# Value outputs at the end of the step, softmax scaling ahead of the next score read, and banks and pieces of the next projection dealt out anew

## The chip, the cores and the metric

The kernel runs on one core of a Trainium2 chip. The metric is device time in microseconds (us) of one execution, and lower is better. The kernel is one launch of hand-ordered instruction streams: TensorE (PE in the profile), VectorE (DVE), ScalarE (ACT), GpSimd (POOL) and the DMA queue of SyncE (SP). Each engine runs its own stream in order and waits on semaphores for the others.

## The reference

One layer of a hybrid attention block over 1024 frames of width 1024, then a SwiGLU and a last norm. Cut to what matters here:

```python
h = rmsnorm(x); proj = h @ w_in
# A: 4 heads, two softmax maps each; a = p0 - lam*p1; o = a @ v (v 128 wide)
# B: 8 heads of 64, band of 9 chunks of 64 keys; o = softmax(q k^T/8 + bias) @ v
# C: 8 heads of 64, causal, score += c_q - c_k; o = softmax(...) @ v
merged = sum_i sigmoid(gate_i) * (o_i @ w_br_i)
x = x + merged @ w_out
x = x + (silu(h2 @ w_gate) * (h2 @ w_up)) @ w_down
return rmsnorm(x)
```

All of it is float32. The kernel gets float32 precision out of TensorE by splitting each operand into a high and a low part (`_hi`, `_lo`) and adding three products (`three_passes`, L182 to L184).

## The kernel before, in words

The program is four blocks: norm, attention, merge and feed-forward. Only the attention block is touched. It runs 12 **units**: four of branch A (one head with its two maps each), four of B and four of C (two heads each). The units of A and of B are two bodies in a loop of two turns, those of C are written out.

Within a unit there are 16 **steps**. Step s has one query tile of 128 rows and one map or head. The four engines do this for step s:

- **TensorE** multiplies the scores of step s + 2 (L927, L928, in C also the mask, L930), turns the probabilities of step s by transposes through the identity (L956; in A only in odd steps), does some **pieces** of the next unit's projection (L182 to L184; a piece is 6 matmuls of 512 columns), and in even steps from 2 on multiplies by V (L972 and L974 in A, L993 and L994 in B and C).
- **VectorE** reads the scores out of PSUM with the bias added and the row's extreme (`read_scores`, L780; in C one more small operation, L789), divides the next step's probabilities by their sum (`scale_probs`, L811 and L813; in A instead `mix_maps`, L820 to L825, in even steps), and subtracts for the low part of the turned chunks (`chunks_low`, L798 and L801).
- **ScalarE** takes the high part of the turned chunks (`chunks_hi`, L663 and L665) and the exponentials of step s + 2 (`exp`, L650).
- The **value output** of a product by V is a copy on ScalarE (`o_low_a` L674, `o_low_bc` L682) and an addition on VectorE (`o_out_a` L836, `o_out_bc` L846). It comes in odd steps from 3 on.

The next unit's projection is 6 **groups** g0 to g5 of 4 pieces: g0 and g1 give K, g2 and g3 give Q, g4 and g5 give V. g0 is done ahead of step 0, the rest at the steps of `PIECES_AT`. `EVAC_AT` says at which step ScalarE (`project_out`) and, for K and Q, VectorE (`project_low`, L742 to L751) empty a group, and `SPLIT_AT` at which step ScalarE makes the high part of the next weight slab (`split_hi`, L616), after which GpSimd makes its low part (`split_lo`, L589). TensorE begins a group once its PSUM bank is free and its slab is split. Both waits stand in `piece`. The bank of a group is chosen in `proj_bank`; banks 0 and 1 hold the scores of even steps and 2 and 3 those of odd steps, and a step of 4 key tiles or fewer leaves the second bank of its pair unused.

In the loop of a step the value output stands first on both engines, and on VectorE the next score read stands ahead of the scaling (L865 to L878).

Of the kernel before, what the change touches and what calls it, by code (L numbers as in the profile page):

```python
# [32 lines left out]
P = 128  # L33
# [82 lines left out]
PIECES_AT = [2, 2, 2, 2, 0, 2, 2, 0, 2, 2, 0, 1, 1, 1, 1, 0, 0]  # L116
EVAC_AT = {0: 0, 2: 1, 4: 2, 7: 3, 10: 4, 16: 5}
SPLIT_AT = {0: 1, 5: 2, 10: 3}
# [298 lines left out]
def block_attention(nc, ps, keep, scratch, w_in_k, w_br_b):  # L417
    h_hi, h_lo, ident = keep["h_hi"], keep["h_lo"], keep["ident_r"][:, :].bitcast(F32)
    with ExitStack() as ctx:
# [23 lines left out]
        neg_max, shift, rowsum, rinv = (sb(n, [P, 4]) for n in ("neg_max", "shift", "rowsum", "rinv"))  # L443
# [32 lines left out]
        def proj_bank(unit, g):  # L476

            if isinstance(unit, int) and unit in (0, UNITS):
                return bank(ps, (0, 1, 2, 3, 5, 6)[g] if unit == 0 else 6)
            return bank(ps, (3, 1, 6, 6, 6, 6)[g])  # L480
# [131 lines left out]
        def _(act):  # L612
# [57 lines left out]
            def o_low_a(c, i):  # L670

                act.wait_ge(pv_chunk, c["chunks"] + chunks_through(0, 2 * i + 1))
                act.wait_ge(rinv_ready, c["outs"] + (i + 1))
                nc.scalar.activation(o_low[:, i % 2 * P:(i % 2 + 1) * P], pv_bank[:, P:2 * P], ACT.Copy,  # L674
                                     scale=rinv[:, 2 * (i % 2):2 * (i % 2) + 1]).then_inc(o_low_ready, 1)
# [8 lines left out]
            def unit_body(b, it, du, last=False):  # L684
# [7 lines left out]
                for s in range(STEPS + 2):  # L692
                    if b == 0 and s >= 3 and s % 2 == 1:
                        o_low_a(c, (s - 3) // 2)
                    if b > 0 and s >= 3 and s % 2 == 1:
                        o_low_bc(c, (s - 3) // 2)
# [16 lines left out]

# [21 lines left out]
        def _(dve):  # L735
# [79 lines left out]
            def mix_maps(c, i):  # L815
# [4 lines left out]
                nc.vector.reciprocal(rinv[:, q:q + 2], rowsum[:, q:q + 2]).then_inc(rinv_ready, 1)  # L820
                dve.wait_ge(rinv_ready, c["outs"] + (i + 1))
                nc.vector.tensor_scalar(ratio[:, i % 2:i % 2 + 1], rowsum[:, q:q + 1], rinv[:, q + 1:q + 2],
# [9 lines left out]
            def o_out_a(c, i):  # L832
                if i == 0:
                    heads_room(c)
                dve.wait_ge(o_low_ready, c["outs"] + (i + 1))
                nc.vector.scalar_tensor_tensor(out=heads[:, i * P:(i + 1) * P], in0=pv_bank[:, 0:P],  # L836
                                               scalar=rinv[:, 2 * (i % 2):2 * (i % 2) + 1], in1=o_low[:, i % 2 * P:(i % 2 + 1) * P],
                                               op0=ALU.mult, op1=ALU.add).then_inc(o_out, 1)
# [10 lines left out]
            def unit_body(b, it, du, project=True):  # L849
# [14 lines left out]
                for s in range(STEPS + 2):  # L864
                    if b == 0 and s >= 3 and s % 2 == 1:  # L865
                        o_out_a(c, (s - 3) // 2)
                    if b > 0 and s >= 3 and s % 2 == 1:
                        o_out_bc(c, (s - 3) // 2)
                    if b == 0 and s % 2 == 0 and s < STEPS:
                        mix_maps(c, s // 2)  # L870
                    if project and s in EVAC_AT:
                        project_low(c["unit"] + 1, EVAC_AT[s], 1 - du)
                    if s + 2 < STEPS:
                        read_scores(b, c, s + 2)
                    if b > 0 and s + 1 < STEPS:
                        scale_probs(b, c, s + 1)
                    if s in turns:
                        chunks_low(b, c, s)  # L878
# [15 lines left out]
        def _(pe):  # L894
            def piece(unit, n, slot):
# [6 lines left out]
                if part == 0 and not (isinstance(unit, int) and unit == 0):  # L902
                    pe.wait_ge(proj_out, 6 * unit + g)
# [6 lines left out]
            def score(b, c, s, last):  # L910
# [9 lines left out]
                if s == STEPS // 2 and not last:  # L920
                    pe.wait_ge(proj_out, 6 * c["unit"] + 8)
# [57 lines left out]
            def times_v_bc(b, c, g):  # L979
                i, m = 2 * (g // 2), g % 2  # L980
                first, n = keys_of(b, g)
                if g >= 2:
                    pe.wait_ge(o_out, c["outs"] + (g - 1))
                elif b == 1 and g == 0:
                    pe.wait_ge(o_out, c["outs"])
# [864 lines left out]
```

## Time and profile before

| | us |
|---|---|
| median of 3 runs | 2151.11 |
| lowest and highest of them | 2147.57 and 2158.26 |
| the profiled execution | 2156.16 |
| its span, first to last instruction | 2154.3 |
| TensorE busy in it | 1988.8 (92%) |
| VectorE busy | 999.7 (46%) |
| ScalarE busy | 710.8 (33%) |
| GpSimd busy | 94.5 (4%) |

The attention block lies between 86 and 917 us of the span. In the rows further down, a bracket at a row's end is the time for which the engine had stood idle before it, and the instruction of another engine whose end released it. Matmuls are pipelined: one of 512 columns is shown with 0.39 us although the next one starts 0.23 us after it, so the time that a wait costs is best read between starts of rows.

### The profile page before, as it was taken

The numbers are of one execution on the slowest core, as the hardware profiler recorded it, in microseconds if no ns is written. First come the engines' busy times: TensorE is split into PE (matmuls) and PEld (weight loads), VectorE is DVE, ScalarE is ACT, GpSimd is POOL, SyncE is SP. The second block draws the span as 40 slices with busy tenths as digits, with TensorE's granted clock in tenths as the row PEclk, the third lists the DMA queues.
The fourth block names the chain that finished last, engine by engine and source line by source line (L and its number), as shares of the span: only waits on it lengthen the run. The fifth ranks groups of instructions, "written<-read, shape, count | busy, mean of one in ns | idle before, by whom it ended". The sixth has DMA issues, their size and how long they took to land. (4 is left out here: it accounts for less than half of the span.)

```text
span 2154.3 us, 26265 instructions
## 1 busy us (share of the span) xinstructions
PE 1988.8 (92%) x9542; PEld 1647.9 (76%) x9542; DVE 999.7 (46%) x1950; ACT 710.8 (33%) x1310; POOL 94.5 (4%) x59
## 2 busy tenths in 40 slices
PE   7888988888888888899999999999999999999997
PEld 3777777777777777778787887878888888888886
DVE  4355555565556556732433225754333333333326
ACT  5344444554545445522233112241111111111122
POOL 1110100100100000000000000000000000000000
PEclk9999999999999999999999999999999999999998
DMA  6412222122212211031211113102111111111111
GB/s 218 127 50 50 75 64 61 43 50 61 68 49 50 69 53 31 30 118 44 83 45 53 49 44 147 59 20 59 59 49 31 47 49 58 49 49 29 49 59 78
DMA packets 145268, 133.32 MB, mean 62 GB/s; under 512 B 7476, under 2 KB 130484, under 8 KB 142888
## 3 DMA queue, kind: packets, MB, share of 16 engines
q1 hardware_dynamic: 141768, 132.16, 20.8%
q8 instruction: 44, 0.72, 0.1%
q10 hardware_dynamic: 3424, 0.17, 0.1%
q14 instruction: 32, 0.26, 0.0%
HBM read 109.17 MB, written 16.06 MB: 58 GB/s over the span
## 5 line engine op out<-in xcount | busy, mean ns | idle before, releaser
L182 PE MATMUL ps<-h_hi,w_hi 128*128 128x512 f32 x1664 | 674.3, 405 | 51.2 <-DVE k_stack L745 37.4
L184 PE MATMUL ps<-h_hi,w_lo 128*128 128x512 f32 x1664 | 658.9, 396 | 0.0
L183 PE MATMUL ps<-h_lo,w_hi 128*128 128x512 f32 x1664 | 658.8, 396 | 0.0
L182 PEld LDWEIGHTS ps<-h_hi,w_hi 128*128 128x128 f32 x1664 | 318.8, 192 | 121.9 <-DVE k_stack L745 37.0
L184 PEld LDWEIGHTS ps<-h_hi,w_lo 128*128 128x128 f32 x1664 | 318.7, 192 | 69.5
L183 PEld LDWEIGHTS ps<-h_lo,w_hi 128*128 128x128 f32 x1664 | 319.6, 192 | 62.0
L1598 DVE TENSOR_TENSOR residual<-residual,ps 128x512 f32<-128x512 f32 x240 | 162.6, 685 | 113.9 <-PE ps L184 109.2
L956 PE MATMUL ps<-ident_r,probs_bc 128*128 128x128 f32 x528 | 85.2, 285 | 51.9 <-DVE probs_bc L813 36.3
L1589 DVE TENSOR_TENSOR w_lo<-w_raw,w_hi 128x1024 fp32r<-128x1024 f32 x46 | 56.4, 1226 | 158.4 <-ACT w_hi L1491 158.4
L1499 ACT ACTIVATE bias<-ps 128x512 f32<-128x512 f32 x44 | 26.1, 594 | 311.5 <-PE ps L184 311.5
L184 PE MATMUL ps<-w_down_hi,act_lo 128*128 128x512 f32 x320 | 124.5, 389 | 0.0
L183 PE MATMUL ps<-w_down_lo,act_hi 128*128 128x512 f32 x320 | 124.5, 389 | 0.0
L182 PE MATMUL ps<-w_down_hi,act_hi 128*128 128x512 f32 x320 | 124.5, 389 | 0.0
L589 POOL TENSOR_TENSOR w_lo<-w_raw,w_hi 128x1024 fp32r<-128x1024 f32 (+1 forms) x36 | 85.2, 2368 | 723.0 <-ACT w_hi L616 690.3
L780 DVE CUSTOM_DVE_ANT_0 probs_bc<-ps,bias 128x640 f32<-128x640 f32 (+7 forms) x128 | 90.0, 703 | 53.5 <-PE ps L930 24.2
L956 PEld LDWEIGHTS ps<-ident_r,probs_bc 128*128 128x128 f32 x528 | 60.1, 143 | 66.4 <-DVE probs_bc L813 40.8
L1607 DVE TENSOR_TENSOR bias<-ps,bias 128x512 f32<-128x512 f32 x44 | 30.4, 691 | 167.2 <-PE ps L184 167.2
L665 ACT ACTIVATE probs_tb_hi<-ps 128x384 fp32r<-128x384 f32 (+2 forms) x192 | 82.6, 463 | 74.0 <-PE ps L956 72.6
L927 PE MATMUL ps<-k_stack,q_stack 128*128 128x320 f32 (+5 forms) x288 | 98.3, 345 | 0.0
L928 PE MATMUL ps<-k_stack,q_stack 128*128 128x320 f32 (+5 forms) x288 | 95.5, 335 | 0.0
L1504 ACT ACTIVATE act_hi<-bias 128x512 fp32r<-128x512 f32 x44 | 27.8, 632 | 202.9 <-DVE bias L1607 202.9
L801 DVE TENSOR_TENSOR probs_tb_lo<-ps,probs_tb_hi 128x384 fp32r<-128x384 f32 (+2 forms) x192 | 93.8, 516 | 2.1 <-ACT probs_tb_hi L665 1.7
(202 smaller groups left out, 2714.9 us busy)
## 6 DMA issues: line engine op xcount, KB each, us to landing
w_raw<-in_w_in SPq DMA_DIRECT2D x60, 512.0 KB, 3.8
w_raw<-in_w_gate_up SPq DMA_DIRECT2D x44, 512.0 KB, 3.7
k_stack<-k_stack SPq DMA_DIRECT2D x24, 512.0 KB, 6.4
w_raw<-in_w_down SPq DMA_DIRECT2D x22, 512.0 KB, 3.5
x_all<-in_x SPq DMA_DIRECT2D x8, 512.0 KB, 8.7
bias<-bias_a_scratch SPq DMA_DIRECT2D x4, 1024.0 KB, 5.9
heads_bc_scratch<-heads_out SPq DMA_DIRECT2D x8, 512.0 KB, 3.1
bias<-neg_c_scratch SPq DMA_DIRECT2D x4, 1024.0 KB, 5.3
```

The source lines that it names most:

```text
L182: nc.tensor.matmul(out, w_hi, x_hi, start=first, stop=False)
L183: nc.tensor.matmul(out, w_hi, x_lo, start=False, stop=False)
L184: return nc.tensor.matmul(out, w_lo, x_hi, start=False, stop=last)
L589: nc.gpsimd.tensor_tensor(w_lo[part], w_raw[part], w_hi[part].bitcast(F32), ALU.subtract).then_inc(w_split, 1)
L665: nc.scalar.activation(turned_place(ptb_hi, b, i, m, tile, size), turn_bank[lc % 2][:, 0:size * P].rearrange("p (t q) -> p t q", q=P), ACT ...
L780: nc.vector.tensor_tensor_reduce(out=row_view(probs_of(b, s)[:, 0:n * P], n), in0=scores_view(s, n), in1=row_view(window, n), scale=-1.0, ...
L801: nc.vector.tensor_tensor(turned_place(ptb_lo, b, i, m, tile, size), turn_bank[lc % 2][:, 0:size * P].rearrange("p (t q) -> p t q", q=P), ...
L927: nc.tensor.matmul(dst, q, k_st[:, par, 2 * m, keys], start=True, stop=False)
L928: last_one = nc.tensor.matmul(dst, q, k_st[:, par, 2 * m + 1, keys], start=False, stop=not diagonal)
L956: last = nc.tensor.transpose(turn_bank[lc % 2][:, x * P:(x + 1) * P], src[:, tile * P:(tile + 1) * P], ident[:, :])
L1589: nc.vector.tensor_tensor(w_lo[kind], w_raw[:, raw, :], w_hi[kind].bitcast(F32), ALU.subtract).then_inc(w_split, 1)
L1598: nc.vector.tensor_tensor(res[:, t, cols], res[:, t, cols], bank(ps, 4 + o % 4), ALU.add).then_inc(added, 1)
```

## The change

The arithmetic and the number of instructions on data stay as they are. What moves:

1. ScalarE's copy and VectorE's addition of the value output go from the head of an odd step to its end. `rinv` grows from 4 to 8 columns so that A's two reciprocals live long enough.
2. In B and C, VectorE scales the probabilities of step s + 1 ahead of reading the scores of step s + 2.
3. The groups g0 to g5 go to banks 3, 6, 1, 6, 6, 6 (before 3, 1, 6, 6, 6, 6), and a group waits only for the last group of its own bank to be emptied, where before it waited for all groups ahead of it.
4. Pieces, emptyings and slab splits are dealt out anew over the steps.
5. A product by V in B and C waits until the output just ahead of it is out (`outs + g`, before `outs + g - 1` from g = 2 on).

```diff
-PIECES_AT = [2, 2, 2, 2, 0, 2, 2, 0, 2, 2, 0, 1, 1, 1, 1, 0, 0]
-EVAC_AT = {0: 0, 2: 1, 4: 2, 7: 3, 10: 4, 16: 5}
-SPLIT_AT = {0: 1, 5: 2, 10: 3}
+PIECES_AT = [2, 2, 2, 2, 1, 1, 1, 1, 0, 1, 1, 1, 1, 1, 1, 2, 0]
+EVAC_AT = {0: 0, 2: 1, 4: 2, 8: 3, 13: 4, 16: 5}
+SPLIT_AT = {0: 1, 4: 2, 8: 3}
+PROJ_BANKS = (3, 6, 1, 6, 6, 6)
...
-        neg_max, shift, rowsum, rinv = (sb(n, [P, 4]) for n in ("neg_max", "shift", "rowsum", "rinv"))
+        neg_max, shift, rowsum = (sb(n, [P, 4]) for n in ("neg_max", "shift", "rowsum"))
+        rinv = sb("rinv", [P, 8])
...
-            return bank(ps, (3, 1, 6, 6, 6, 6)[g])
+            return bank(ps, PROJ_BANKS[g])
...
                 for s in range(STEPS + 2):
-                    if b == 0 and s >= 3 and s % 2 == 1:
-                        o_low_a(c, (s - 3) // 2)
-                    if b > 0 and s >= 3 and s % 2 == 1:
-                        o_low_bc(c, (s - 3) // 2)
...
                         split_hi(slab + j, odd % 2, 6 * b + 3 * it + odd // 2)
-
+                    if b == 0 and s >= 3 and s % 2 == 1:
+                        o_low_a(c, (s - 3) // 2)
+                    if b > 0 and s >= 3 and s % 2 == 1:
+                        o_low_bc(c, (s - 3) // 2)
...
                 for s in range(STEPS + 2):
+                    if b == 0 and s % 2 == 0 and s < STEPS:
+                        mix_maps(c, s // 2)
+                    if project and s in EVAC_AT:
+                        project_low(c["unit"] + 1, EVAC_AT[s], 1 - du)
+                    if b > 0 and s + 1 < STEPS:
+                        scale_probs(b, c, s + 1)
+                    if s + 2 < STEPS:
+                        read_scores(b, c, s + 2)
+                    if s in turns:
+                        chunks_low(b, c, s)
                     if b == 0 and s >= 3 and s % 2 == 1:
                         o_out_a(c, (s - 3) // 2)
                     if b > 0 and s >= 3 and s % 2 == 1:
                         o_out_bc(c, (s - 3) // 2)
-                    if b == 0 and s % 2 == 0 and s < STEPS:
-                        mix_maps(c, s // 2)
-                    if project and s in EVAC_AT:
-                        project_low(c["unit"] + 1, EVAC_AT[s], 1 - du)
-                    if s + 2 < STEPS:
-                        read_scores(b, c, s + 2)
-                    if b > 0 and s + 1 < STEPS:
-                        scale_probs(b, c, s + 1)
-                    if s in turns:
-                        chunks_low(b, c, s)
...
-                    pe.wait_ge(proj_out, 6 * unit + g)
+                    same = [x for x in range(g) if PROJ_BANKS[x] == PROJ_BANKS[g]]
+                    pe.wait_ge(proj_out, 6 * unit + (same[-1] + 1 if same else 0))
...
-                    pe.wait_ge(proj_out, 6 * c["unit"] + 8)
+                    pe.wait_ge(proj_out, 6 * c["unit"] + 9)
...
-                if g >= 2:
-                    pe.wait_ge(o_out, c["outs"] + (g - 1))
-                elif b == 1 and g == 0:
-                    pe.wait_ge(o_out, c["outs"])
+                pe.wait_ge(o_out, c["outs"] + g)
```

Two places show what stands in a row. The first is VectorE in the first B unit, from the end of step 6 to the low part of step 7. L813 is the scaling, L780 the score read, L801 the low part of turned chunks, L846 the value output, L748 and L751 the low part of g3 (Q). Before:

```order
L846 TENSOR_TENSOR heads_out<-ps,o_low 64x256 [waits o_low_ready]
L740 REGISTER_ALU
L748 SCALAR_TENSOR_TENSOR q_stack<-ps,q_stack 64x512 [waits proj_hi]
L750 REGISTER_ALU
L751 SCALAR_TENSOR_TENSOR q_stack<-ps,q_stack 64x512 [waits proj_hi]
L771 REGISTER_ALU
L780 ISA probs_bc,neg_max<-ps,bias 128x640 [waits scores_ready,chunk_turned]
L780 ISA neg_max 128x1
L811 RECIPROCAL rinv<-rowsum 128x1 [waits probs_ready]
L812 REGISTER_ALU
L813 TENSOR_SCALAR probs_bc<-probs_bc,rinv 128x640 [waits rinv_ready]
```

and now (lines from here on are numbered one to three higher in the changed kernel):

```order
L812 RECIPROCAL rinv<-rowsum 128x1 [waits probs_ready]
L813 REGISTER_ALU
L814 TENSOR_SCALAR probs_bc<-probs_bc,rinv 128x640 [waits rinv_ready]
L772 REGISTER_ALU
L781 ISA probs_bc,neg_max<-ps,bias 128x640 [waits scores_ready,chunk_turned]
L781 ISA neg_max 128x1
L797 REGISTER_ALU
L802 TENSOR_TENSOR probs_tb_lo<-ps,probs_tb_hi 128x4x128 [waits chunk_hi]
L847 REGISTER_ALU
L848 TENSOR_TENSOR heads_out<-ps,o_low 64x256 [waits o_low_ready]
L741 REGISTER_ALU
L749 SCALAR_TENSOR_TENSOR q_stack<-ps,q_stack 64x512 [waits proj_hi]
```

The scaling has moved from behind the value output, g3 and the score read to the head of the step; the value output has moved behind the chunks; and g3 belongs to step 8 now.

The second place is TensorE in the same unit at step 8: the transposes of step 8, then what comes ahead of the product by V. Before:

```order
L954 REGISTER_ALU
L956 MATMUL ps<-ident_r,probs_bc 128x128 [waits chunk_out]
L956 MATMUL ps<-ident_r,probs_bc 128x128
L901 REGISTER_ALU
L903 REGISTER_ALU [waits w_split]
L182 MATMUL ps<-h_hi,w_hi 128x512 [waits proj_out]
L183 MATMUL ps<-h_lo,w_hi 128x512
```

and now:

```order
L957 REGISTER_ALU
L959 MATMUL ps<-ident_r,probs_bc 128x128 [waits chunk_out]
L959 MATMUL ps<-ident_r,probs_bc 128x128
L985 REGISTER_ALU
L993 MATMUL ps<-probs_tb_hi,v_split 128x256 [waits chunk_out,o_out]
L994 MATMUL ps<-probs_tb_lo,v_split 128x256
```

The two pieces of step 8 are gone from there (one each has gone to steps 4 and 7, and the others moved along), so the product by V stands right behind the transposes.

## Rows read from the trace of the kernel before

**Rows 1.** Waits on TensorE: waiter, releaser, us in total, times, longest us.

```profile
PE ps L182 <- DVE k_stack L745: 37.4, 22, 1.9
PE ps L956 <- DVE probs_bc L813: 36.3, 21, 3.2
PE ps L956 <- DVE probs_tb_lo L801: 15.3, 17, 1.4
```

**Rows 2.** Windows: stretch, then PE, PEld, DVE, ACT, POOL busy, granted clock, DMA.

```profile
150.00:218.00 68.00, 60.57 (x314) 51.09 (x313) 36.87 (x86) 32.26 (x68) 7.43 (x4) 0.95 0.24 67
351.00:419.00 68.00, 57.40 (x331) 48.97 (x329) 40.34 (x106) 34.79 (x79) 7.59 (x5) 1.00 0.21 56
711.00:790.00 79.00, 67.29 (x370) 57.83 (x369) 47.09 (x122) 37.52 (x79) 7.16 (x3) 0.94 0.19 54
921.00:2154.00 1233.00, 1206.10 (x5328) 996.09 (x5328) 473.72 (x638) 262.30 (x358) 0.00 (x0) 0.99 0.19 57
```

**Rows 3.** Timeline of TensorE, first B unit: start us, us, then instruction.

```profile
354.48 0.30 PE L956 MATMUL ps<-ident_r,probs_bc 128*128 128x128 f32 x1
356.58 0.50 PE L182 MATMUL ps<-h_hi,w_hi 128*128 128x512 f32 x1 [1.80 <-DVE k_stack L745]
359.41 0.28 PE L927 MATMUL ps<-k_stack,q_stack 128*128 128x256 f32 x1
...
364.89 0.50 PE L182 MATMUL ps<-h_hi,w_hi 128*128 128x512 f32 x1 [1.65 <-DVE k_stack L745]
...
375.11 0.66 PE L956 MATMUL ps<-ident_r,probs_bc 128*128 128x128 f32 x4 [1.70 <-DVE probs_bc L813]
...
387.19 0.96 PE L956 MATMUL ps<-ident_r,probs_bc 128*128 128x128 f32 x5 [2.46 <-DVE probs_bc L813]
...
396.11 0.71 PE L956 MATMUL ps<-ident_r,probs_bc 128*128 128x128 f32 x5
396.58 0.37 PE L993 MATMUL ps<-probs_tb_hi,v_split 128*128 128x256 f32 x1
...
398.01 0.36 PE L927 MATMUL ps<-k_stack,q_stack 128*128 128x320 f32 x1
...
415.96 0.27 PE L927 MATMUL ps<-k_stack,q_stack 128*128 128x128 f32 x1
```

**Rows 4.** Timeline of VectorE, same unit, steps 6 and 7.

```profile
380.27 1.17 DVE L813 TENSOR_SCALAR probs_bc<-probs_bc,rinv 128x512 f32<-128x512 f32 x1
...
383.52 0.42 DVE L846 TENSOR_TENSOR heads_out<-ps,o_low 64x256 f32<-64x256 f32 x1 [1.62 <-ACT o_low L682]
...
385.56 0.82 DVE L780 CUSTOM_DVE_ANT_0 probs_bc<-ps,bias 128x640 f32<-128x640 f32 x1
...
386.50 0.55 DVE L813 TENSOR_SCALAR probs_bc<-probs_bc,rinv 128x640 f32<-128x640 f32 x1
```

**Rows 5.** Timelines of ScalarE and GpSimd, same unit.

```profile
357.29 1.04 ACT L616 ACTIVATE w_hi<-w_raw 128x1024 fp32r<-128x1024 f32 x1
386.42 0.83 ACT L650 ACTIVATE probs_bc<-probs_bc,neg_max 128x640 f32<-128x640 f32 x1 [1.08 <-DVE neg_max L780]
387.16 0.18 ACT L650 ACTIVATION_READ_ACCUMULATOR probs_bc<-probs_bc,neg_max 128x1 f32 x1
```
```profile
358.48 2.40 POOL L589 TENSOR_TENSOR w_lo<-w_raw,w_hi 128x1024 fp32r<-128x1024 f32 x1 [24.50 <-ACT w_hi L616]
...
378.76 2.40 POOL L589 TENSOR_TENSOR w_lo<-w_raw,w_hi 128x1024 fp32r<-128x1024 f32 x1 [17.37 <-ACT w_hi L616]
```

**Rows 6.** Timeline of VectorE in the third C unit, 8 key tiles.

```profile
844.17 1.21 DVE L780 CUSTOM_DVE_ANT_0 probs_bc<-ps,bias 128x1024 f32<-128x1024 f32 x1
...
845.42 0.27 DVE L789 TENSOR_SCALAR shift<-neg_max,c_col 128x1 f32<-128x1 f32 x1
```

**Rows 7.** Timeline of TensorE, last wait of the first A unit.

```profile
145.10 0.39 PE L972 MATMUL ps<-v_split,probs_ta_hi 128*128 128x256 f32 x1 [1.05 <-DVE probs_ta_lo L798]
```

**Rows 8.** Timeline of TensorE, last unit (C), a late wait.

```profile
907.90 1.05 PE L956 MATMUL ps<-ident_r,probs_bc 128*128 128x128 f32 x7 [1.43 <-DVE probs_tb_lo L801]
```

More of the change, by code:

```diff
@@ L674, in o_low_a @@
                 nc.scalar.activation(o_low[:, i % 2 * P:(i % 2 + 1) * P], pv_bank[:, P:2 * P], ACT.Copy,
-                                     scale=rinv[:, 2 * (i % 2):2 * (i % 2) + 1]).then_inc(o_low_ready, 1)
+                                     scale=rinv[:, 2 * (i % 4):2 * (i % 4) + 1]).then_inc(o_low_ready, 1)
             def o_low_bc(c, g):
@@ L819, in mix_maps @@
                 dve.wait_ge(probs_ready, c["step"] + (2 * i + 2))
-                nc.vector.reciprocal(rinv[:, q:q + 2], rowsum[:, q:q + 2]).then_inc(rinv_ready, 1)
+                r = 2 * (i % 4)
+                nc.vector.reciprocal(rinv[:, r:r + 2], rowsum[:, q:q + 2]).then_inc(rinv_ready, 1)
                 dve.wait_ge(rinv_ready, c["outs"] + (i + 1))
-                nc.vector.tensor_scalar(ratio[:, i % 2:i % 2 + 1], rowsum[:, q:q + 1], rinv[:, q + 1:q + 2],
+                nc.vector.tensor_scalar(ratio[:, i % 2:i % 2 + 1], rowsum[:, q:q + 1], rinv[:, r + 1:r + 2],
                                         keep["neg_lam"][:, :], ALU.mult, ALU.mult).then_inc(ratio_ready, 1)
@@ L836, in o_out_a @@
                 nc.vector.scalar_tensor_tensor(out=heads[:, i * P:(i + 1) * P], in0=pv_bank[:, 0:P],
-                                               scalar=rinv[:, 2 * (i % 2):2 * (i % 2) + 1], in1=o_low[:, i % 2 * P:(i % 2 + 1) * P],
+                                               scalar=rinv[:, 2 * (i % 4):2 * (i % 4) + 1], in1=o_low[:, i % 2 * P:(i % 2 + 1) * P],
                                                op0=ALU.mult, op1=ALU.add).then_inc(o_out, 1)
```

## The prediction

> **What bounds the kernel now.** I read three views in turn. The windows come first [rows 2]. From 921 us on TensorE is busy for 1206 of 1233 us, and nothing there is touched. In the attention block it is busy for only 57 of 68 us in a unit, while VectorE has 40 and ScalarE 35. No engine is full: the block is bound by chains of waits. The waits view names them [rows 1]. TensorE starts a projection group late because K of the group ahead is still being emptied (37.4 us), turns late because the probabilities aren't scaled (36.3), and waits for the low parts of the chunks turned ahead (15.3). The timeline of one B unit then shows the seven waits that each of the four B units has: 1.80 and 1.65 at the starts of g1 and g2, 1.70 and 2.46 at the transposes of steps 5 and 8 [rows 3], and further on 1.31, 0.35 and 1.34 at steps 12, 14 and 16, for low parts. They sum to 10.6 us by the brackets. Between starts a wait is some 0.2 longer: the transpose at 354.48 takes 0.06 to issue, and the next matmul starts at 356.58, so 2.04 are lost where the bracket says 1.80. A B unit thus loses about 12 us. By the same count an A unit loses 9 (7.4 by its brackets) and a C unit 13 (11.7).
>
> A second loss comes with them. The granted clock is 1.00 in the first B unit and 0.94 to 0.95 in the A and the C unit shown [rows 2]; 0.05 of 68 us is 3.4 us. 
>
> **Method.** I keep the durations of the rows and lay them along the new order of each engine, one unit of each kind. The latencies between engines come from the rows too: a score read of 640 columns and its accumulator take 0.83 and an exponential 0.92 until its sum is out [rows 4, 5]; a reciprocal and scaling take 0.74; a TensorE wait ends 0.14 after VectorE (386.50 + 0.55 to 387.19); two pieces take 2.83 (356.58 to 359.41).
>
> **Part 1, banks (change 3).** g1 no longer waits for g0. It starts at 354.54 instead of 356.58. g2 has bank 1 and waits for no group, so the 1.65 goes too. What is late next is the weight slab. ScalarE's high part comes after the exponential of step 2, whose score read now stands behind a scaling; that moves it from 357.29 to 358.05. GpSimd then works 2.40 us, until 361.65 [rows 5], and TensorE, ready at 361.0, starts g2 at 361.8: a new wait of 0.8. Net gain 3.1 in B. In A no scaling stands in front and the wait is 0.35, in C 0.65. Score(8) waits for one more group than before, which is emptied at step 4, and costs nothing.
>
> **Part 2, the middle of the unit (changes 1, 2 and 4).** At step 5 the 1.70 goes: one piece (1.45) now lies in front, and the scaling saves itself the score read (0.6 to 0.8). At step 8 the 2.46 goes for the same reasons, g3 being emptied one step later. But the new order makes a chain on VectorE and ScalarE: score read, exponential, scaling, next score read. One turn of it is 0.83 + 0.92 + 0.74 and 0.06 of signals, 2.55 us; in odd steps the value output hangs behind the exponential (copy 0.38, addition 0.43) and adds 0.84. A pair of steps takes 5.94. TensorE needs 6.3 for a pair with one piece in each (two scores 1.2, transposes 2 × 0.47 from 396.11 to 396.58, a product 1.43 from there to 398.01, pieces 2.8 [rows 3]). So the chain fits, with 0.4 to spare, except where something else is put in. At step 8 it is: g3 costs VectorE 1.4 and ScalarE 1.2, TensorE has no piece there, and the product now waits for the output just ahead of it (change 5). Laid out, B waits 0.65 at the product of step 6, 0.6 and 1.0 at step 8 (second chunk; product), and 2.0 at the transposes of step 9. From step 10 on it waits 0.1 in all.
>
> **Part 3, the end of the unit.** The 1.31 and 0.35 go because VectorE no longer stands still for the value output before the low parts. The 1.34 goes because two pieces (2.83) lie between the last transposes and the last product, which needs only some 2.2.
>
> **Sum for B:** new waits 0.8 + 0.65 + 0.6 + 1.0 + 2.0 + 0.1 = 5.1 for 12.1, a gain of 7.0 a unit, 28 for four.
>
> **C:** the chain is longer. At 8 tiles the read with its shift is 1.52 [rows 6], the exponential 1.26 and the scaling 0.96; a pair of such steps takes 8.4, and TensorE needs at most 8.1 for its own pair, so there the chain leads. New waits: 0.65, 0.5, 0.9 + 1.05 at step 8, 2.1 at step 9, then 0.3, 0.15, 0.3 and 1.45 at step 14, in all 7.4 for 13.2. Gain 6, for three units 18. **The last unit** has few pieces, and VectorE and ScalarE set its pace already; a late wait for a low part there is 1.43 [rows 8]. There the longer chain shows: its last exponential comes some 3 us later. I take −2.5.
>
> **A:** there is no scaling in A; only the value output moves. It has a single PV bank, so each product waits for the output ahead of it, which now comes after the low part and an exponential instead of before them. With one piece a step the cover is thinner. I lay out 0.35 (slab), 0.3, 1.6 at step 8, 0.85 for g4 (its bank is freed at step 8 now), 1.8 at step 10, 0.25, 2.0 for g5 at step 13 (ScalarE empties g4 behind an exponential), 0.1: 7.2 for 9. The last wait, 1.05 for the low part [rows 7], goes, the middle pays. Gain 2, for four units 8.
>
> **Clock:** the waits at g1 go, which start 7 of the 17 falls. But the new waits lie close together at steps 8 to 10, and I expect a fall there in most units. From 17 to about 14: +4. The bounds are +20 (hardly any fall left) and −10 (two in each unit).
>
> Together: 28 + 18 − 2.5 + 8 + 4 = 55.5 us. The profiled execution (2156.2) would become 2100.7; it lies 5 above the median, so the forecast is 2151.1 − 55.5 = **2095.6**. Errors of 1.5 us a unit either way, which the closeness of chain and TensorE makes likely, are 17 us: 2079 to 2113.
>
> **Rivals.** (a) *GpSimd holds the scaling up.* The scaling at 380.27 took 1.17 for 512 columns where a longer one takes 0.55, and ended 0.28 after the slab split that began at 378.76 [rows 4, 5]. The scaling is on the chain now. In my layout the three splits miss it by 0.1 to 0.5 us in most steps; if they hit, up to 2.4 us less a scaling's own 0.5 is paid, once a unit at least: 8 × 2 = 16 to 30 us of gain lost, time 2112 to 2126. The Trainium skill (SBUF — State Buffer, the contention rules) calls this an exclusive lock on a port pair that VectorE and GpSimd share, the second to come waiting in full; by that rule the hit costs the whole rest of the split, as the row shows.
>
> (b) *The waits only change their name.* If ScalarE's queue is later than I laid out (each copy and exponential behind another), steps 8 to 10 lose 4 to 5 us more in each unit and the sum is 0 to 10: 2141 to 2151. For it: the chain has only 0.4 us to spare in B and none in C. Against it: both engines are busy for under 60% [rows 2].
>
> (c) *Slower.* The product by V now waits for the output just ahead. The path score read, exponential, copy, addition, signals is 3.25 us in B and TensorE's cover is 4.3. It decides from the point where VectorE lags by more than that 1 us at every odd step: then each of the seven products pays the lag. At 1.5 us, 10 us a unit against gains of 2 to 7, about +40 us: 2190.
>
> **Chances.** Forecast 2079 to 2113: 0.66. Better still, with the clock back: 0.08, 2062 to 2079. (a) 0.13. (b), with 2126 to 2140 halved between it and (a): 0.08. (c) 0.05. The range that leaves 0.2 out is 2078 to 2124. A measurement of this kernel can tell about 0.5% (11 us) from no change: faster (below 2140) 0.88, within 0.07, slower 0.05.
>
> **What would show each step.** In the changed trace no wait for K at L745 stands before a projection matmul; in its place a wait of 0.3 to 0.8 for GpSimd's w_lo at g2. Waits for the scaling (L814) are gone from step 5 and small at step 8, and waits for L848 or the low part stand at steps 6, 8 and 9. In A waits for the value output stand at steps 8 and 10 and for ScalarE's V copy at step 13. The B units take 61 to 63 us and C units 69 to 72; the last unit is longer than its 52. It would be wrong if A lost time, if scalings of over 1 us stood on the path, or if TensorE waited at every product.

## The result: 2073.8 us, 3.8% below the kernel before

The median of four runs is 2073.84 us (2073.59 to 2074.27). The kernel before had 2154.69 beside it (four runs, 2147.57 to 2161.72). The ratio is 0.9625, 95% interval 0.9590 to 0.9661. The gain is 81 us where 55.5 were forecast, and the time lies 5 us below the range, in the class to which the prediction gave 0.08. The profiled execution has a span of 2071.8 us against 2154.3, so the two traces differ by 82.5.

The page of the changed kernel, its span and its line of busy times:

```profile
span 2071.8 us, 26269 instructions
PE 1967.5 (95%) x9542; PEld 1634.1 (79%) x9542; DVE 1007.4 (49%) x1950; ACT 703.7 (34%) x1310; POOL 94.1 (5%) x59
```

TensorE's busy time fell from 1988.8 to 1967.5 although it runs the same matmuls. With it the mean granted clock rose from 0.980 to 0.988. The rest is waiting that went. The waits of TensorE (line waited at, line that ended it, total, times, longest; six rows of the attention block and the merge's first wait), against [rows 1]:

```profile
PE ps L959 <- DVE probs_tb_lo L802: 21.5, 22, 2.2
PE ps L993 <- DVE heads_out L848: 13.1, 15, 2.1
PE ps L975 <- DVE heads_out L838: 9.4, 8, 1.6
...
PE ps L183 <- DVE w_lo L1223: 4.7, 1, 4.7
...
PE ps L959 <- DVE probs_bc L814: 4.0, 2, 3.2
...
PE ps L183 <- ACT gate_first L627: 3.2, 5, 0.7
PE ps L183 <- POOL w_lo L591: 3.0, 10, 0.4
```

The 37.4 us for K (L745 before) have no row any more. The 36.3 us for the scaling are 4.0 in 2 waits: one at the turn of B's loop (0.8), and one at the start of the last unit (3.2), which was there before too. New are the value outputs, 13.1 + 9.4 us.

The timeline of TensorE in the first B unit, to be read against [rows 3] (only the rows with a wait between the starts of g2 and step 9):

```profile
338.51 0.50 PE L183 MATMUL ps<-h_hi,w_hi 128*128 128x512 f32 x1 [0.28 <-POOL w_lo L591]
...
357.34 0.44 PE L959 MATMUL ps<-ident_r,probs_bc 128*128 128x128 f32 x2 [0.15 <-DVE probs_tb_lo L802]
358.55 0.39 PE L993 MATMUL ps<-probs_tb_hi,v_split 128*128 128x256 f32 x1 [0.77 <-DVE heads_out L848]
...
362.25 0.77 PE L959 MATMUL ps<-ident_r,probs_bc 128*128 128x128 f32 x5 [1.92 <-DVE probs_tb_lo L802]
```

These four are all the waits of that unit: 3.1 us by their brackets, where the unit before had 10.6. The first A unit has five, 3.5 us for 7.4:

```profile
97.15 0.50 PE L183 MATMUL ps<-h_hi,w_hi 128*128 128x512 f32 x1 [0.27 <-POOL w_lo L591]
...
115.14 0.38 PE L975 MATMUL ps<-v_split,probs_ta_hi 128*128 128x256 f32 x1 [0.78 <-DVE heads_out L838]
117.79 0.50 PE L183 MATMUL ps<-h_hi,w_hi 128*128 128x512 f32 x1 [0.19 <-DVE q_stack L752]
...
123.21 0.38 PE L975 MATMUL ps<-v_split,probs_ta_hi 128*128 128x256 f32 x1 [1.56 <-DVE heads_out L838]
...
133.64 0.50 PE L183 MATMUL ps<-h_hi,w_hi 128*128 128x512 f32 x1 [0.72 <-ACT gate_first L627]
```

Why the 1.92 at step 9 stands is seen on VectorE, in the same stretch:

```profile
358.08 0.42 DVE L848 TENSOR_TENSOR heads_out<-ps,o_low 64x256 f32<-64x256 f32 x1 [0.79 <-ACT o_low L684]
358.69 0.68 DVE L749 SCALAR_TENSOR_TENSOR q_stack<-ps,q_stack 64x512 fp32r<-64x512 f32 x1 [0.20 <-ACT q_stack L632]
359.39 0.69 DVE L752 SCALAR_TENSOR_TENSOR q_stack<-ps,q_stack 64x512 fp32r<-64x512 f32 x1
...
360.31 0.55 DVE L814 TENSOR_SCALAR probs_bc<-probs_bc,rinv 128x640 f32<-128x640 f32 x1
360.90 0.82 DVE L781 CUSTOM_DVE_ANT_0 probs_bc<-ps,bias 128x640 f32<-128x640 f32 x1
...
361.65 0.88 DVE L802 TENSOR_TENSOR probs_tb_lo<-ps,probs_tb_hi 128x384 fp32r<-128x384 f32 x2
```

The value output and both halves of g3 stand ahead of scaling, score read and low part. From 358.08 VectorE works with a gap of only 0.20 us, and TensorE is let go by the low part at its end.

**Where the 82.5 us lie.** A unit's length is the time from its first eight V transposes to the next unit's; the last one's runs to the merge's first matmul (its 57.1 thus counts the merge's 4.7 us wait, which the prediction's "52" left out). A fall is a stretch at half clock (0.50 granted). In each of them the clock that is missing, one minus the granted clock summed over the stretch, comes to 1.7 us.

| kind | before, us (falls) | after, us (falls) | difference |
|---|---|---|---|
| A, 4 units | 64.3 (0), 67.4 (2), 65.7 (1), 67.3 (2) | 60.3, 60.3, 60.2, 60.3 (0) | −23.6 |
| B, 4 units | 68.5 (0), 71.5 (2), 70.1 (1), 70.0 (1) | 60.6 (0), 60.7 (0), 62.7 (1), 60.8 (0) | −35.3 |
| C, first 3 | 79.5 (3), 79.0 (3), 75.0 (2) | 69.1 (1), 69.1 (1), 65.8 (0) | −29.5 |
| last unit | 57.1 | 62.3 | +5.2 |
| ahead of them, and from the merge on | | | +0.7 |

Units of one kind that differ only by a fall differ by 1.5 us (A: 64.3, 65.7, 67.3 with 0, 1, 2 falls), so 1.6 a fall was right. The falls in the first eleven units went from 17 to 3 (a second profile of the changed kernel has 4, one of them of double length, so 3 is a good draw). With 1.6 us for each, the 88.4 us of these units part into 22 of clock and 66 of waits: 16 in A, 30 in B, 20 in C. The last unit and the start of the merge have half clock too: two stretches of 1.7 us before, and two of 1.7 and one of 5.1 after. The longest lies about the merge's wait of 4.7 us, where TensorE has nothing to run.

### The profile page after: what moved, and what is told of

Read it like the earlier page. It is cut to its first block and busy times, and to the rows that moved or that the text cites. A ratio compares the mean times of both kernels' runs of the same rounds, so it can differ in the third digit from the quotient of the medians.

```text
span 2071.8 us, 26269 instructions
## 1 busy us (share of the span) xinstructions
PE 1967.5 (95%) x9542; PEld 1634.1 (79%) x9542; DVE 1007.4 (49%) x1950; ACT 703.7 (34%) x1310; POOL 94.1 (5%) x59
## 5 line engine op out<-in xcount | busy, mean ns | idle before, releaser
L959 PE MATMUL ps<-ident_r,probs_bc 128*128 128x128 f32 x528 | 84.3, 282 | 25.8 <-DVE probs_tb_lo L802 21.5
```

The source lines that it names most:

```text
L959: last = nc.tensor.transpose(turn_bank[lc % 2][:, x * P:(x + 1) * P], src[:, tile * P:(tile + 1) * P], ident[:, :])
```

## The experiments

One profile shows one draw of the falls. The kernel before was run 42 times beside the experiments; its time goes with its mean granted clock: 2156.9 us at 0.980 (13 runs), 2153.3 at 0.982 (13), 2150.6 at 0.983 (6), 2146.4 at 0.986 (2). That is 1.9 us for each 0.001 of this kernel (used for the others it is an estimate), and the reason why this kernel spreads over 17 us (2144.9 to 2162.2) and the changed one over 1 to 4. Each kernel is therefore shown with its mean clock over its runs. The kernel before has 0.9815, the changed one 0.988 (0.987 on a second chip).

| kernel | median, us | ratio, 95% interval | mean clock |
|---|---|---|---|
| changed | 2073.8 | 0.9625 (0.9590 to 0.9661) | 0.988 |
| before + change 3 alone | 2098.2 | 0.9748 (0.9714 to 0.9782) | 0.988 |
| changed without change 3 | 2126.1 | 0.9876 (0.9841 to 0.9911) | 0.985 |
| changed without change 4 | 2117.2 | 0.9833 (0.9799 to 0.9867) | 0.977 |
| changed without change 1 | 2131.2 | 0.9887 (0.9853 to 0.9922) | 0.982 |
| changed without change 2 | 2070.4 | 0.9603 (0.9570 to 0.9636) | 0.990 |
| before, matmuls in the waits at g1, g2 | 2155.5 | 0.9999 (0.9976 to 1.0022) | 0.985 |
| the same, and at step 5 | 2148.5 | 0.9980 (0.9965 to 0.9996) | 0.986 |

### The banks alone, and all but the banks

The kernel before with change 3:

```diff
-            return bank(ps, (3, 1, 6, 6, 6, 6)[g])
+            return bank(ps, (3, 6, 1, 6, 6, 6)[g])
...
-                    pe.wait_ge(proj_out, 6 * unit + g)
+                    pe.wait_ge(proj_out, 6 * unit + (0, 0, 0, 2, 4, 5)[g])
...
-                    pe.wait_ge(proj_out, 6 * c["unit"] + 8)
+                    pe.wait_ge(proj_out, 6 * c["unit"] + 9)
```

> The kernel before with change 3 alone (banks 3, 6, 1, 6, 6, 6, a group waits only for its own bank). Per unit the waits at g1 and g2 (about 3.8 us between starts) go and a wait for the slab's low part of 0.3 comes: 3.4 us for 11 units, 37 us. With the clock theory also the 7 falls that begin there, 11 us: 48 us in all, 2103 to 2108. Rival without the clock: 2114 to 2118.

Measured: 2098.22 us, 5 below the range with the clock and 16 below the one without it. Nearly 56 of the 81 us come from two numbers in a table and the wait that goes with them. The first A unit is 60.2 us, as short as with the whole change. The other three are 61.5 to 61.7 with one fall each, which the changed kernel has not. In waits, then, A gains no more by the whole change than by the banks alone. Of the first A unit's waits, the slab at g2 and Q at g4, rows of TensorE's timeline:

```profile
95.95 0.50 PE L182 MATMUL ps<-h_hi,w_hi 128*128 128x512 f32 x1 [0.27 <-POOL w_lo L589]
113.64 0.50 PE L182 MATMUL ps<-h_hi,w_hi 128*128 128x512 f32 x1 [0.83 <-DVE q_stack L751]
```

B units are 65 to 67, C 69 to 74, the last 57.1. The clock over its four runs is 0.988, that of the whole change: by the 1.9 us per 0.001 about 13 of the 56 are clock, and 43 are waits (an estimate): eleven units, each rid of nearly 4 us at g1 and g2.

The changed kernel with the old banks (`PROJ_BANKS = (3, 1, 6, 6, 6, 6)`) and the old wait:

> The changed kernel with change 3 undone: the banks 3, 1, 6, 6, 6, 6 and each group waiting for all groups ahead of it. The waits at g1 and g2 come back, 3.4 us for 11 units, 37 us: 2111. With the clock theory they also bring back some 7 falls, 11 us: 2122. g3 also waits for g2 at step 4 now, where one piece covers little of it: up to 2 us a unit more.

Measured: 2126.05 us, 52 above the changed kernel and 4 above the expectation with the clock; the 2 us a unit that were kept open for g3 can cover it. The waits for K are back with the very sum of [rows 1], and groups further on wait for Q as well:

```profile
PE ps L183 <- DVE k_stack L746: 37.4, 22, 1.9
PE ps L183 <- DVE q_stack L752: 17.2, 15, 1.7
```

### The old deal of pieces

The changed kernel with `PIECES_AT`, `EVAC_AT` and `SPLIT_AT` of before:

> The changed kernel with change 4 undone: pieces, emptyings and slab splits at their old steps (none at steps 4, 7 and 15). Theory of the prediction: at step 5 a wait of 0.9 comes back, at step 8 some 1.5, at the last product 1.3, and the jam at step 9 gets shorter: about 2.5 us a unit, 25 to 30 us, 2100. Rival (the deal matters little, the order on VectorE does the work): within 8 us of the changed kernel, 2066 to 2082.

Measured: 2117.22 us, 43 above the changed kernel where 25 to 30 were expected, and the lowest clock of all, 0.977. TensorE again has no cover at steps 5 and 8:

```profile
357.65 0.66 PE L959 MATMUL ps<-ident_r,probs_bc 128*128 128x128 f32 x4 [1.22 <-DVE probs_bc L814]
369.49 0.54 PE L959 MATMUL ps<-ident_r,probs_bc 128*128 128x128 f32 x3 [2.18 <-DVE probs_bc L814]
370.88 0.44 PE L959 MATMUL ps<-ident_r,probs_bc 128*128 128x128 f32 x2 [0.85 <-DVE probs_tb_lo L802]
395.97 0.47 PE L993 MATMUL ps<-probs_tb_hi,v_split 128*128 128x256 f32 x1 [1.69 <-DVE heads_out L848]
```

2.18 and 0.85 lie 1.4 us apart, the case that the forecast for the clock had in mind. Behind the pair or its first wait a fall begins in three of the four B units. But one begins behind the single wait of 1.69 in three of four as well, and in the unit shown that is the only one. So these rows don't show that it takes waits close together. The B units are 65.2 to 66.9 us (mostly 61 in the changed kernel). Here too a scaling meets the split, one in each B and C unit (1.73 to 1.76 us), which doubles the mean of those of 512 columns (0.52 in the changed kernel). Whether it delays TensorE isn't shown: VectorE stands idle for 1.0 us between it and the scaling for which TensorE waits 2.18.

```profile
L814 DVE TENSOR_SCALAR probs_bc<-probs_bc,rinv 128x512 f32<-128x512 f32 x16 | 16.8, 1049 | 0.6
```

### The place of the value outputs

The changed kernel with `o_low_a`, `o_low_bc`, `o_out_a` and `o_out_bc` back at the head of the step:

> The changed kernel with change 1 undone: copy and addition of the value output at the head of odd steps on ScalarE and VectorE, all else as changed. Theory: VectorE stands for the product again (up to 2 us in each odd step) before it scales, reads and makes low parts; the waits for low parts come back, 2 to 3 us a unit: 2095 to 2110. In exchange the products of steps 6 and 8 no longer wait for the output (about 1 us a unit). Rival (change 1 is worth nothing in B and C because the chain leads): 2070 to 2080.

Measured: 2131.19 us, 57 above the changed kernel and 21 above the top of what was expected. In the changed order the output ahead of the scaling stops the whole chain; the first B unit:

```profile
367.02 0.78 PE L959 MATMUL ps<-ident_r,probs_bc 128*128 128x128 f32 x3 [2.49 <-DVE probs_bc L814]
...
378.71 0.77 PE L959 MATMUL ps<-ident_r,probs_bc 128*128 128x128 f32 x5 [2.19 <-DVE probs_tb_lo L802]
384.35 1.33 PE L959 MATMUL ps<-ident_r,probs_bc 128*128 128x128 f32 x5 [2.91 <-DVE probs_tb_lo L802]
```

In all TensorE waits there 48.9 us for low parts (21.5 in the changed kernel) and 21.6 for the scaling (4.0).

Part of the reason was not expected here. VectorE's scaling and GpSimd's slab split at that place:

```profile
365.26 1.64 DVE L814 TENSOR_SCALAR probs_bc<-probs_bc,rinv 128x384 f32<-128x384 f32 x1
```

```profile
364.34 2.34 POOL L591 TENSOR_TENSOR w_lo<-w_raw,w_hi 128x1024 fp32r<-128x1024 f32 x1 [11.70 <-ACT w_hi L618]
```

A scaling of 384 columns takes 0.42 in the changed kernel; here it takes 1.64 and ends 0.22 after the split. It is rival (a), come true in an experiment: a second one in the same unit takes 1.77 for 0.55, and each of the seven B and C units has the pair, 2.4 us a unit, 17 us in all. For the first of them the rows show that TensorE pays it: its wait of 2.49 ends with the held scaling. B is 68.3 to 68.8 us with one or two falls. A, which has no scaling, loses 2.5 us a unit and more; its wait for ScalarE's V copy at g5 is 2.16 us for 0.72. So the held scalings are not the whole.

So of the three parts 52, 43 and 57 us are lost when one is undone, 152 in sum, for a gain of 81. They don't add up. A likely reason, argued and not tested, is that they share one chain: the banks and the deal bring TensorE early to its transposes, and that is worth something only if VectorE isn't held.

### Scaling ahead of the score read

```diff
+                    if s + 2 < STEPS:
+                        read_scores(b, c, s + 2)
                     if b > 0 and s + 1 < STEPS:
                         scale_probs(b, c, s + 1)
-                    if s + 2 < STEPS:
-                        read_scores(b, c, s + 2)
```

> The changed kernel with change 2 undone: VectorE reads the scores of step s + 2 ahead of scaling the probabilities of step s + 1. Theory of the prediction (read, exponential and scaling form a chain that leads in C and in the last unit): the chain is broken, so the last unit gets back 5 us and C about 1 a unit, while the scaling at step 5 comes 0.6 later for 7 units and shows 0 to 0.5 of it: 2064 to 2074. Rival (scaling first is a gain): 2080 to 2095.

Measured: 2070.36 us, 3.5 below the changed kernel, as expected. Change 2 is worth nothing on the whole. The four B units take 246.7 us without it and 244.9 with it, with one fall in either sum: 0.4 us a unit. The three C units, where 1 us each was expected back, are as long as with it (69.1, 69.1, 66.0). The one wait of step 9 is split in two (1.79 and 1.28). But the comparison isn't a clean one. Without change 2 scalings meet splits again, two in each B unit and three in each C unit, and take 2.0 to 2.5 us each (1.5 in one case). The row of step 9's wait for the low part, and the scaling and the split ahead of it in the first B unit:

```profile
363.80 0.77 PE L959 MATMUL ps<-ident_r,probs_bc 128*128 128x128 f32 x5 [1.28 <-DVE probs_tb_lo L802]
```

```profile
360.81 2.47 DVE L814 TENSOR_SCALAR probs_bc<-probs_bc,rinv 128x640 f32<-128x640 f32 x1
```

```profile
360.54 2.39 POOL L591 TENSOR_TENSOR w_lo<-w_raw,w_hi 128x1024 fp32r<-128x1024 f32 x1 [9.42 <-ACT w_hi L618]
```

The scaling takes 2.47 us for 0.55, the low part follows it without a gap, and TensorE waits for that. So the gain of change 2 in B, and its tie in C, may be nothing but splits that it makes the scalings miss. Reading first with the splits placed so that the scalings miss them was not run; it could be faster than both.

The last unit, where only one short split is left, is 57.38 instead of 62.26. There few pieces cover anything, and the scaling stands in the way of the read on which the exponential hangs. Two of the last unit's waits at products in the changed kernel:

```profile
790.87 0.39 PE L993 MATMUL ps<-probs_tb_hi,v_split 128*128 128x256 f32 x1 [2.10 <-DVE heads_out L848]
...
803.18 0.38 PE L993 MATMUL ps<-probs_tb_hi,v_split 128*128 128x256 f32 x1 [0.88 <-DVE heads_out L848]
```

and with the read first, where they are 1.03 and 0.22:

```profile
792.03 0.39 PE L993 MATMUL ps<-probs_tb_hi,v_split 128*128 128x256 f32 x1 [1.03 <-DVE heads_out L848]
...
802.02 0.38 PE L993 MATMUL ps<-probs_tb_hi,v_split 128*128 128x256 f32 x1 [0.22 <-DVE heads_out L848]
```

### What lets the clock fall

The windows of TensorE in the second A unit of the kernel before (columns: window, its length, busy times and counts of PE, PEld, DVE, ACT, POOL, then the granted clock):

```profile
154.00:156.00 2.00, 0.33 (x3) 0.12 (x1) 1.23 (x2) 1.18 (x2) 0.00 (x0) 1.00 0.00 0
156.00:158.00 2.00, 1.80 (x5) 1.47 (x6) 0.58 (x3) 1.36 (x3) 0.00 (x0) 0.69 0.00 0
158.00:160.00 2.00, 2.00 (x6) 1.56 (x5) 0.00 (x0) 0.19 (x1) 1.67 (x1) 0.50 0.00 0
```

and matmuls in it:

```profile
156.20 0.50 PE L182 MATMUL ps<-h_hi,w_hi 128*128 128x512 f32 x1 [1.87 <-DVE k_stack L745]
...
156.77 0.62 PE L184 MATMUL ps<-h_hi,w_lo 128*128 128x512 f32 x1
157.19 0.63 PE L182 MATMUL ps<-h_hi,w_hi 128*128 128x512 f32 x1
...
160.18 0.40 PE L183 MATMUL ps<-h_lo,w_hi 128*128 128x512 f32 x1
```

After the wait of 1.87 us TensorE runs at 1.00 for some 0.6 us; from 156.77 on the starts lie 0.43 apart instead of 0.23, until 160.18. Eight matmuls lose 0.2 us each: the 1.6 us of a fall, seen singly. To test whether the waits do it, seven matmuls were put ahead of the waits at g1 and g2, where 7 of the 17 falls had begun (6 and 1; the 10 in the expectation is too many). They write the bank that the group behind them overwrites, so they change no result and only keep TensorE at work.

```diff
+                if part == 0 and g in (1, 2) and not (isinstance(unit, int) and unit == 0):
+                    fill(proj_bank(unit, g), 7)
                 if part == 0 and g % 2 == 0:
                     pe.wait_ge(w_split, 3 * unit + (j + 1))
```

> The kernel before, with only the seven matmuls ahead of the waits at g1 and g2, and nothing at step 5; their results are overwritten. Clock theory: the falls that began at g1 and g2 (10 of the 17 in the first eleven units) don't come, and those at steps 5, 8 and 9 stay or come back: some 7 falls, A units 64.3 to 65.7, B 69 to 70, C 75 to 77.5; 2143 us if no stall between loops comes, as it came once with the fillers at step 5. Rival (idle time elsewhere brings them as well once the clock has recovered: falls only move): 13 or more falls, and the time of the kernel before or above.

The same place in its profile:

```profile
154.82 1.78 PE L898 MATMUL ps<-h_hi 128*128 128x512 f32 x7
156.86 0.50 PE L182 MATMUL ps<-h_hi,w_hi 128*128 128x512 f32 x1 [0.26 <-DVE k_stack L745]
...
154.00:156.00 2.00, 2.00 (x12) 1.67 (x11) 0.89 (x2) 1.19 (x2) 0.00 (x0) 1.00 0.19 76
156.00:158.00 2.00, 1.74 (x8) 1.14 (x7) 1.22 (x4) 0.70 (x4) 0.00 (x0) 1.00 0.00 0
158.00:160.00 2.00, 2.00 (x13) 1.68 (x11) 0.00 (x0) 0.85 (x1) 1.00 (x1) 1.00 0.00 0
```

The group starts no earlier, and no fall comes. In the first eleven units of this profile 6 falls are left for 17, none at g1 or g2: the A units take 64.3, 64.3, 64.1 and 65.6, as the one unit without a fall did before. So a fall at these places comes from the idle time there: filled, with K as late as ever, 22 waits brought none, where 7 came before. How many falls it saves in all is less sure, for this profile is a good draw (2143.8 us at 0.987) and the one of before a poor one. Over ten runs the clock is 0.985 for 0.9815, which is some 4 falls a run (an estimate: 0.0035 of 2150 us, 1.7 us each). The time is another matter. The median of the ten is 2155.5 us, no gain, where 2143 was expected. At 0.988 a line through these ten runs lies 2.5 us above one through the 42 of before, and at their own mean clock they are some 5 above it. Where the rest goes isn't settled. The rival was right on the time and wrong on the count.

With six more matmuls ahead of the transposes of step 5, in bank 1:

> The kernel before, with idle TensorE time filled: 7 extra matmuls of 512 columns ahead of the waits at the starts of g1 and g2 in every unit, and 6 ahead of the scaling's wait at step 5 in B and C. Their results are overwritten. They take about as long as the waits of 1.7 to 1.9 us that they lie in (0.23 us each), so without the clock they change the time by -2 to +8 us. If the falls to 1.2 GHz come from TensorE idling at those waits, 8 to 10 of the 17 falls of the attention block go, and the time drops by 10 to 16 us against the kernel before, although TensorE does more work. Rival (falls come whatever these waits are): no faster than before.

Measured: 2148.49 us, ratio 0.998, clock 0.986. That is a gain of 5 us where 10 to 16 were expected. Its profile has no fall at g1, g2 or step 5. Three of those left in the first eleven units begin at step 8 in B and C, behind the wait of 2.45 or 2.58 that nothing fills. The longest lies about two stalls in one B unit that no semaphore explains, near the turn of the loop, of which this is the longer:

```profile
483.80 0.58 PE L935 MATMUL ps<-k_stack,q_stack 128*128 128x256 f32 x1 [2.87 <-issue]
```

That unit took 76.6 us for 68.6. The cause of the stalls is open; the changed kernel has no such row in its attention block.

### The last unit, and g3 emptied later

The last unit alone in its old order, everything (value outputs first, read first):

> The changed kernel, with the old order in the last unit alone (value outputs first, score read ahead of the scaling). The last unit took 57.1 us from its first V transpose to the merge block's first matmul before and 62.3 after. Theory: it goes back to 57, and the kernel to 2068 to 2070. Rival (the last unit is longer for what it inherits from the unit ahead or from the clock): it stays at 61 to 63, the kernel at 2073.

Measured: 2070.24 us (2068.27 to 2071.00), clock 0.989; the last unit 57.37. Since that is what the read alone had given, it was tried apart, beside the changed kernel on the same chip:

> The changed kernel unaltered, on the chip of the next run, so that a difference of some 3 us can be told. 2073 to 2075 us; no theory differs here.

> The changed kernel, with change 2 undone in the last unit alone (there VectorE reads the next scores ahead of the scaling, the value outputs stay last). Theory (all that the last unit lost comes from the scaling standing ahead of the read, and B gains some 0.7 us a unit by it): last unit 57.4, other units as in the changed kernel, 2069 us, 5 below the changed kernel on this chip. Rival (the last unit's loss hangs on the state of the clock at its start and on the value outputs as well): last unit 60 or more, 2072 to 2074.

Measured, five runs each: 2075.63 (2074.04 to 2077.86) and 2068.78 us (2067.53 to 2072.92), ratios to before 0.9637 (0.9609 to 0.9664) and 0.9599 (0.9573 to 0.9626). The last unit is 57.42 for 62.28. Change 2 in the last unit explains nearly all of its loss (4.9 of 5.2), and this is the fastest version of the study, 6.9 us under the changed kernel, of which 4.9 is that unit; the rest goes with the clock (0.989 for 0.987).

Then g3's emptying at step 8 was put behind the exponential and the low part, on both engines, on top of the last unit's old order: first in all units, then in B and C alone.

```diff
-                    if project and s in EVAC_AT:
+                    if project and s in EVAC_AT and (b == 0 or s != 8):
                         project_low(c["unit"] + 1, EVAC_AT[s], 1 - du)
...
                     if s in turns:
                         chunks_low(b, c, s)
+                    if b > 0 and project and s == 8:
+                        project_low(c["unit"] + 1, EVAC_AT[s], 1 - du)
```

> last_old, and in step 8 of all other units the emptying of g3 stands behind the exponential on ScalarE and behind the low parts on VectorE instead of at the head of the step. Theory: the jam at steps 8 and 9 (2.8 us in B, 4 in C) comes from g3's 1.4 us on VectorE and 1.2 on ScalarE on the chain; with g3 behind, the wait at the transposes of step 9 (1.9 to 2.2) falls by 1 or more, but g4 can start only once g3 is out and waits up to 1: 0.5 to 1.5 us a unit better than last_old, 2053 to 2064. Rival (g4's wait takes all of it): equal to last_old or slower.

> The last unit in its old order, and Q of g3 emptied behind the exponential and the low parts of step 8 in B and C alone; A keeps the order of the changed kernel. Theory (gain and loss are local to a unit): A units at 60.3 us, B units at 60.9 without a fall of the clock, C units near 68 to 69, last unit 57.1; 2066 us, and the best so far by 4. Rival (what is won in B is lost elsewhere, as in the run with all units changed, or falls come at other places): 2070 to 2074.

Measured: 2073.88 and 2070.11 us, against 2070.24. The rival held both times. The wait moves from step 9 to the start of g4, here in the first of the two runs:

```profile
369.16 0.50 PE L183 MATMUL ps<-h_hi,w_hi 128*128 128x512 f32 x1 [1.62 <-DVE q_stack L758]
```

In A it is 2.6 us there, a fall follows in each A unit, and each takes 61.9 for 60.3. In B and C alone nothing is won: 1.62 at g4 stands for 1.92 at step 9, and two of four B units have a fall there.

## Why the prediction was wrong

The direction, the mechanism and most of the places were right. The sum was short by 27 us of the two profiles' 82.5, and two terms carry it: the clock, and the waits of A. With either as forecast the time would have lain just inside the range, some 2082 us (an estimate: 2073.8 and 8).

- **The clock, the largest miss.** The step that failed is "I expect a fall there in most units. From 17 to about 14: +4". Three were left (4 in the second profile, one of double length), 22 us instead of 4 in the first eleven units. Over all runs the shift from 0.9815 to 0.988 is 12.5 us (1.9 per 0.001; the profiled run of before had 0.980, a poor draw by 3 us), so by that measure the term was short by 8 and not by 18. The mean also counts the last unit and the merge's start, where the changed profile has 5.1 us of clock missing that the other hasn't, in good part while TensorE waits; so the truth is likely between the two. The range's bound "+20 (hardly any fall left)" was about what came, but the range's width of 17 was made of errors in the waits alone. What failed was the belief that 0.8 and 1.9 us at steps 8 and 9 would do what 1.9 and 1.8 did at g1 and g2. In A they never did, in B in one unit of four (three of four in the second profile of the changed kernel), in C in two of three.
- **A, a gain of 2 a unit.** It was 4: 16 us for 8. Laid out were 0.35, 0.3, 1.6, 0.85, 1.8, 0.25, 2.0 and 0.1, in all 7.2; measured 0.27, 0, 0.78, 0.19, 1.56, 0, 0.72 and 0, 3.5 by the brackets and some 4.5 between starts. The waits of the middle were thus priced at more than twice what they cost; which duration or order in the layout made them so isn't shown. "The middle pays" was right: with change 3 alone a unit without a fall has the same length, the three waits at its end (1.09, 0.56, 1.05) standing for those at the products and at g5 (0.78, 1.56, 0.72). So changes 1 and 4 together bring A nothing. The new place of the value outputs is needed there all the same: with it undone A loses 2.5 us a unit.
- **B, 7.0 a unit.** It was 7.6, 30 us for 28. The slab cost 0.28 for 0.8, the product of step 6 nothing for 0.65, the second chunk of step 8 0.15 for 0.6, its product 0.77 for 1.0, and the transposes of step 9 took 1.92 for 2.0. Steps 12 to 16 have no wait, as said.
- **C, 6 a unit.** It was 6.6, 20 us for 18. Its waits are 0.37, 0.44, 0.66 + 0.88, 2.22 and 0.43 in the first two units; of the 1.45 at step 14 there is 0.43, and 0.94 in the third.
- **The last unit, −2.5.** It was −5.2, of which 4.9 come from change 2, as the last runs show. The cause was named ("there the longer chain shows") and its price halved.
- **Change 2 in B.** Part 2 counted "the scaling saves itself the score read (0.6 to 0.8)" at steps 5 and 8. It brings 0.4 in a unit, 1.8 us in four, and that perhaps only by the splits that it misses; and it takes 4.9 in the last. As a part of the change it is a loss.

The sum in numbers: 82.5 − 55.5 = 27; clock +18.4, A +7.6, B +2.5, C +1.9, last unit −2.7, ahead and behind −0.7.

**The rivals.** (a) GpSimd hardly held the scaling in the changed kernel. Those of 640 columns got shorter, from a mean of 617 ns to 554, none above 0.56 us:

```profile
L814 DVE TENSOR_SCALAR probs_bc<-probs_bc,rinv 128x640 f32<-128x640 f32 x40 | 22.2, 554 | 1.4
```

Of 512 columns, where [rows 4] has one of 1.17 us, five touch the end of a split and take 0.55 to 0.67 us for 0.49. In the kernel before each of the four B units has two scalings of 1.16 to 1.20. Otherwise the splits miss the scalings, as laid out. That hangs on the order of everything: with change 1, 2 or 4 undone, or change 3 made alone, scalings are held; with change 3 undone they aren't. With change 1 or 2 undone held ones stand on the path, as shown. The port rule of the Trainium skill (SBUF — State Buffer, Who interferes with whom) says that the first to start keeps the shared ports for its whole instruction. The traces agree: with change 1 undone the held scaling ended 0.22 us after the split that had begun before it. The price named for the rival, 16 to 30 us, was about right: the 17 us of time by which the scalings of that run are longer. (b) was wrong: the waits shrank from 10.6 to 3.1 in B. But with change 1, 3 or 4 undone the time is 2117 to 2131, and 43 to 57 us of the gain are gone. (c) was wrong: in A two products a unit wait for the output ahead (0.78 and 1.56), in B one and in C two, in the last unit, which has few pieces, five, never all seven. Change 5 was not undone by itself.

## What to carry to other kernels

Where a wait is due to the place of a buffer and not to work, look at it first: two entries of a bank table alone were worth 56 us, with 81 for the whole. Price the waits of the bounding engine with the clock that falls behind them, in a term with bounds of its own that the range keeps, and take that term from the clock of many runs, not of one profile. An order that costs nothing where other work covers it can harm where little does: give the last turn of a pipeline its own.

## What the runs showed of the hardware

A wait of TensorE of 1.9 us in a stream that is otherwise dense was followed, within 0.6 to 1.5 us of its end, by some 3 us at half clock (0.50 granted), 1.6 us lost; not each time: the first A unit has the same wait and no fall. Adding 14 matmuls a unit in such waits left A units shorter, 64.1 to 65.6 for 64.3 to 67.4 us, although TensorE had more to do. The spread of this kernel's runs, 17 us, follows the mean granted clock with 1.9 us per 0.001, and the changed kernel, with fewer waits, is also steadier: 4 runs within 0.7 us, 5 on another chip within 3.8. And moving the value output by a few instructions made scalings of 0.42 and 0.55 us take 1.64 and 1.77, since they now began within a slab split of GpSimd; they ended 0.22 and 0.35 us after it.
